# All activation products of a two-block transformer kernel read interleaved halves

## The reference

```
h = rmsnorm(x, norm)
x = x + (silu(h @ w_gate) * (h @ w_up)) @ w_down     # three times, 1024 -> 2816 -> 1024
q, k, v, ... = split(h @ w_in)                       # and the other projections, 1024 wide inputs
```

## Time and profile before

| | |
|---|---|
| Median of three timed runs | 1687.73 us |
| The profiled execution, its own time | 1688.09 us |
| Its span in the trace | 1686.3 us |
| TensorE matmul busy | 1664.0 us, 99% of the span, 10716 matmuls |
| TensorE weight loads busy | 1461.9 us, 87% |
| VectorE, ScalarE, GpSimd busy | 1259.2, 854.7, 527.4 us |
| TensorE clock granted, mean | 0.996 of full speed |

### The profile page before, as it was taken

How to read it: one execution, slowest core, us unless ns; L and a number is a source line. 1 busy time by engine, 2 the same in 40 slices (tenths; PEclk the granted TensorE clock), 3 DMA queues, 4 the chain that set the end, 5 groups by cost and what they waited for, 6 DMA issues and landing times.

```text
span 1686.3 us, 27591 instructions
## 1 busy us (share of the span) xinstructions
PE 1664.0 (99%) x10716; PEld 1461.9 (87%) x10716; DVE 1259.2 (75%) x1752; ACT 854.7 (51%) x1314; POOL 527.4 (31%) x368
## 2 busy tenths in 40 slices
PE   9989999999999999999999999999999999999997
PEld 7867789999998866789999998788888999899886
DVE  7767788845876798788855887688868975488675
ACT  6448457724763322557733774433335673277342
POOL 1451125503540446326502540121502560255000
PEclk9999999999999999999999999999999999999999
DMA  6310223433433565223344333422222333433432
GB/s 223 91 51 2 76 75 105 115 113 94 119 105 104 130 153 141 81 75 101 102 114 112 101 107 97 132 75 75 76 76 75 101 101 113 113 101 92 121 94 81
DMA packets 284923, 169.11 MB, mean 100 GB/s; under 512 B 8336, under 2 KB 278880, under 8 KB 284800
## 3 DMA queue, kind: packets, MB, share of 16 engines
q1 hardware_dynamic: 283792, 165.16, 34.8%
q0 software_dynamic: 720, 1.72, 0.3%
q10 hardware_dynamic: 288, 0.54, 0.1%
HBM read 156.71 MB, written 2.10 MB: 94 GB/s over the span
## 4 chain that ended last, share of the span: by engine, by line
PE 50%; DVE 4%; ACT 1%; issue 1%; DVEq 0%; ACTq 0%
PE ps L1454 22%; PE ps L1104 9%; PE ps L1106 9%; PE ps L1105 9%; DVE w L1803 1%; PE ps L1668 1%; ACT w L640 1%; DVE w L2131 0%; DVE act_lo L1835 0%; DVE bt_lo L1833 0%; DVE rstd L1845 0%; DVE tt L2147 0%; ACT w L810 0%; DVE x L2634 0%; PE ps L1681 0%
## 5 line engine op out<-in xcount | busy, mean ns | idle before, releaser
L1104 PE MATMUL ps<-act_hi,w 128*128 128x512 f32 x788 | 312.8, 397 | 3.8 <-DVE w L1803 2.3
L1106 PE MATMUL ps<-act_hi,w 128*128 128x512 f32 x788 | 307.0, 390 | 0.0
L1105 PE MATMUL ps<-act_lo,w 128*128 128x512 f32 x788 | 306.9, 390 | 0.0
L1454 PE MATMUL ps<-act_hi,w 128*128 128x256 f32 (+1 forms) x1461 | 270.3, 277 | 1.6 <-DVE w L2131 1.1
L640 ACT ACTIVATE w<-raw 128x2048 fp32r<-128x2048 f32 (+2 forms) x102 | 163.1, 1599 | 193.6 <-PE ps L1106 179.7
L1454 PEld LDWEIGHTS ps<-act_hi,w 128*128 128x128 f32 x1461 | 229.2, 188 | 3.3 <-DVE w L2131 1.7
L1803 DVE TENSOR_TENSOR w<-raw,w 128x2048 fp32r<-128x2048 f32 (+2 forms) x93 | 180.8, 1944 | 41.4 <-ACT w L640 41.3
L477 POOL TENSOR_TENSOR raw<-raw 128x512 f32<-128x512 f32 x60 | 81.9, 1365 | 405.4 <-DVE sqacc L1823 164.0
L1104 PE MATMUL ps<-hid_hi,w 128*128 128x512 f32 x528 | 200.1, 379 | 0.0
L1105 PE MATMUL ps<-hid_lo,w 128*128 128x512 f32 x528 | 200.1, 379 | 0.0
L1106 PE MATMUL ps<-hid_hi,w 128*128 128x512 f32 x528 | 200.1, 379 | 0.0
(11 more groups left out here) (430 smaller groups left out, 3595.6 us busy)
## 6 DMA issues: line engine op xcount, KB each, us to landing
raw<-in_ffn_w_gate_dram SPq DMA_DIRECT2D x44, 512.0 KB, 4.0
raw<-in_ffn_w_up_dram SPq DMA_DIRECT2D x44, 512.0 KB, 5.2
raw<-in_w_gate_upffn_dram SPq DMA_DIRECT2D x44, 512.0 KB, 4.5
raw<-in_ffn_w_down_dram SPq DMA_DIRECT2D x32, 384.0 KB, 4.2
raw<-in_conv_w_pw_dram SPq DMA_DIRECT2D x24, 512.0 KB, 5.7
raw<-in_w_in_dram SPq DMA_DIRECT2D x24, 512.0 KB, 4.4
raw<-in_ffn_w_down_dram SPq DMA_DIRECT2D x32, 320.0 KB, 3.7
z<-z SPq DMA_DIRECT2D x30, 262.0 KB, 4.9
```

The costliest lines, as they stand in the source:

```text
L1104: pe.matmul(out, lhs[0], rhs[0], start=start, stop=False)
L1105: pe.matmul(out, lhs[0], rhs[1], start=False, stop=False)
L1106: return pe.matmul(out, lhs[1], rhs[0], start=False, stop=stop)
L1454: ins = pe.matmul(out[:, c], lhs, rhs[:, k, c], start=start and k == 0 and rhs is b_hi and lhs is w_hi, stop=k == Q4 - 1 and lhs is w_lo, ...
```

## The change

Every product with activations now reads the columns in interleaved halves: those of 512 columns (`act_k`, and the embedding's `pf_hi`/`pf_lo`) in two halves of 256, the block products of 256 columns in two halves of 128. The output banks hold the tokens in that order, and each line that takes one out reads it with `in_turn` and writes with `by_half`. `act_hi` and `act_lo` become the two parts of one tile, `bt_hi` and `bt_lo` likewise. `HALVED` and the splitting in two pieces go.

```diff
-HALVED = (2, 3, 4, 7, 10, 12, 16)
...
-        act_hi = sb("act_hi", [P, KD, S], F32R)
-        act_lo = sb("act_lo", [P, KD, S], F32R)
+        act = sb("act", [P, 2, KD, S], F32R)
+        act_hi, act_lo = act[:, 0], act[:, 1]
...
+        def combo_tile(name, k):
+
+            if name in SUMS:
+                return bt[:, :, SUMS.index(name), k]
+            rows, cols = {"B11": (0, 0), "B21": (1, 0), "T4": (0, 1), "B22": (1, 1)}[name]
+            return act[:, :, rows * Q4 + k, cols * HALF:(cols + 1) * HALF]
...
-                dst = (a[:, 0:HALF], t2[:, u % 2, HALF:], t1[:, u % 2, HALF:])[i]
-                act.activation(dst, (c, b, a)[i][:, 0:HALF], ACT.Copy).then_inc(sem("taken"), 1)
+                src = (c, b, a)[i][:, 0:HALF]
+                if i:
+                    dst = by_half((t2, t1)[i - 1][:, u % 2, HALF:])
+                    act.activation(dst, in_turn(src), ACT.Copy).then_inc(sem("taken"), 1)
+                else:
+                    act.activation(a[:, 0:HALF], src, ACT.Copy).then_inc(sem("taken"), 1)
...
             def act_k(k):
-                return act_hi[:, k], act_lo[:, k]
+                return halves(act_hi[:, k]), halves(act_lo[:, k])
...
-                    def product(out, w, name, start, sig, halved=False):
-
-                        b_hi, b_lo = combo(name)
+                    def product(out, w, name, start, sig):
+
                         for k in range(Q4):
                             w_hi, w_lo = w(k)
+                            b_hi, b_lo = (halves(combo_tile(name, k)[:, j]) for j in range(2))
                             for lhs, rhs in ((w_hi, b_hi), (w_hi, b_lo), (w_lo, b_hi)):
-                                pieces = 2 if halved and k == 0 and lhs is w_lo else 1
-                                for i in range(pieces):
-                                    c = slice(i * HALF // pieces, (i + 1) * HALF // pieces)
-                                    ins = pe.matmul(out[:, c], lhs, rhs[:, k, c], start=start and k == 0
-                                                    and rhs is b_hi and lhs is w_hi, stop=k == Q4 - 1 and lhs is w_lo,
-                                                    skip_group_check=True)
+                                ins = pe.matmul(out[:, 0:HALF], lhs, rhs, start=start and k == 0 and rhs is b_hi
+                                                and lhs is w_hi, stop=k == Q4 - 1 and lhs is w_lo,
+                                                skip_group_check=True)
                         ins.then_inc(sig, 1)
...
-            def scaled(dst, src, parts=slice(0, P)):
-
-                ve.tensor_tensor(dst, src[parts, :], rstd[parts, :], ALU.mult).then_inc(bank_free, 1)
+            def scaled(dst, src):
+
+                ve.tensor_tensor(by_half(dst), in_turn(src), by_half(rstd[:, :]), ALU.mult).then_inc(bank_free, 1)
```

More of the change, by code:

```diff
@@ L1769, in ple @@
                     pe.wait_ge(sem("pf_done"), 2)
-                tile(T + 1, 4 * i, lambda k: slot(n, KD + k, P), lambda k: (pf_hi[:, k], pf_lo[:, k]), range(2),
+                tile(T + 1, 4 * i, lambda k: slot(n, KD + k, P), lambda k: (halves(pf_hi[:, k]), halves(pf_lo[:, k])), range(2),
                      panel_done)
@@ L1923, in _ @@
                     src = (second if c else first)("q", i)
-                    ve.scalar_tensor_tensor(out=q_f[:, 2 * i + c], in0=src[:, :], scalar=DH ** -0.5, in1=rstd[:, :],
-                                            op0=ALU.mult, op1=ALU.mult).then_inc(bank_free, 1)
+                    ve.scalar_tensor_tensor(out=by_half(q_f[:, 2 * i + c]), in0=in_turn(src), scalar=DH ** -0.5,
+                                            in1=by_half(rstd[:, :]), op0=ALU.mult, op1=ALU.mult).then_inc(bank_free, 1)
                 if i:
@@ L1976, in _ @@
             ve.wait_ge(panel_done, N0["gate"] + 1)
-            scaled(t3[:, 0], bank(T0["gate"]))
+            ve.tensor_tensor(t3[:, 0], bank(T0["gate"])[:, :], rstd[:, :], ALU.mult).then_inc(bank_free, 1)
             lo(N0["kvs"])
@@ L2076, in pooled @@
                 out, scale = ps[pool_banks[gi]], par[:, COL["pool_scale"] + gi:COL["pool_scale"] + gi + 1]
-                ve.tensor_scalar(act_hi[:, 4 + gi], out[:, :], scale, None, ALU.mult).then_inc(sem("y_hi"), 1)
-                low(act_lo[:, 4 + gi], out[:, :], act_hi[:, 4 + gi], "y_hi", gi + 1, "y_lo", scale)
+                ve.tensor_scalar(by_half(act_hi[:, 4 + gi]), in_turn(out), scale, None, ALU.mult)\
+                    .then_inc(sem("y_hi"), 1)
+                low(by_half(act_lo[:, 4 + gi]), in_turn(out), by_half(act_hi[:, 4 + gi]), "y_hi", gi + 1, "y_lo", scale)
             shift_first(0, 0)
@@ L2185, in gate_first @@
                         ve.wait_ge(sem("up_product"), 6 * seven(u) + 3)
-                        ve.tensor_tensor(t1[:, u % 2, 0:HALF], up_banks(dn, u)[2][:, 0:HALF], rstd[:, 0:HALF], ALU.mult)
+                        ve.tensor_tensor(by_half(t1[:, u % 2, 0:HALF]), in_turn(up_banks(dn, u)[2][:, 0:HALF]),
+                                         by_half(rstd[:, 0:HALF]), ALU.mult)
                     def gate_second(u):
@@ L2191, in gate_second @@
                         half = t1[:, u % 2, HALF:]
-                        seq.link(ve.tensor_tensor(half, half, up_banks(dn, u)[1][:, 0:HALF], ALU.add))
+                        seq.link(ve.tensor_tensor(by_half(half), by_half(half), in_turn(up_banks(dn, u)[1][:, 0:HALF]),
+                                                  ALU.add))
                         ve.tensor_tensor(half, half, rstd[:, HALF:], ALU.mult).then_inc(sem("up_summed"), 1)
@@ L2198, in up_second @@
                         half = t2[:, u % 2, HALF:]
-                        ve.tensor_tensor(half, half, up_banks(dn, u)[0][:, 0:HALF], ALU.add).then_inc(sem("c22_set"), 1)
+                        ve.tensor_tensor(by_half(half), by_half(half), in_turn(up_banks(dn, u)[0][:, 0:HALF]), ALU.add)\
+                            .then_inc(sem("c22_set"), 1)
                     def hidden(u, n):
@@ L2218, in whole_hidden @@
                         ve.wait_ge(sem("silu_ready"), u + 1)
-                        for half, sig in ((slice(0, HALF), "up_summed"), (slice(HALF, S), "hidden_set")):
-                            ve.tensor_tensor(t1[:, j, half], up_bank[:, half], t3[:, j, half], ALU.mult)\
+                        for h, sig in enumerate(("up_summed", "hidden_set")):
+                            half = slice(h * HALF, (h + 1) * HALF)
+                            ve.tensor_tensor(t1[:, j, half], in_turn(up_bank)[:, h], t3[:, j, half], ALU.mult)\
                                 .then_inc(sem(sig), 1)
@@ L2458, in _ @@
                     src = (second if c else first)("qk2", i)
-                    ve.scalar_tensor_tensor(out=dst[:, c], in0=src[:, :], scalar=1.0 if i else GDK ** -0.5,
-                                            in1=rstd[:, :], op0=ALU.mult, op1=ALU.mult).then_inc(bank_free, 1)
+                    ve.scalar_tensor_tensor(out=by_half(dst[:, c]), in0=in_turn(src), scalar=1.0 if i else GDK ** -0.5,
+                                            in1=by_half(rstd[:, :]), op0=ALU.mult, op1=ALU.mult).then_inc(bank_free, 1)
             lo(N0["v2"] + 1)
```

37 lines of the change are left out of this document (20 added, 17 removed).

## The result

The changed kernel takes 1661.85 us (median of four runs, 1659.99 to 1663.38), beside 1688.32 us (1687.16 to 1689.13) for the kernel before on the same chip: a ratio of 0.984, 95% interval 0.9827 to 0.9854. In a second session the pair stood at 1658.06 and 1688.26 us, 0.9829 (0.9814 to 0.9844). The forecast was 1655 us, in a range of 1640 to 1675. So the change saves 26.5 us in the first session and 30.2 in the second, where 32.5 had been worked out. The profiled execution took 1661.55 us, its span 1659.7.

What follows compares the result with a forecast made beforehand. TensorE, with matmuls in flight 99% of the span, was taken as the bound. 27.3 + 8.4 + 2.4 - 3.3 - 1.3 - 1.0 = 32.5 us off 1688.1 gave 1655.6, predicted as 1655 us, range 1640 to 1675.

Steps and rivals of the forecast that it cites:

- Products of 512 columns, 27.3 us: 2412 matmuls on `act` and `pf` go from 227.2 to 215.9 ns each, saving 27.3 us.
- Products of 256 columns, 8.4 us: 5040 block products go to 112.1 ns, from 113.2 or, for 620 of them, a slow 117.9: 8.4 us saved.
- The rival of 109.3 ns: Block products of 256 columns run at array speed, 109.3 ns, giving 1641 us; chance 0.14.
- the pace that sticks: Block products gain nothing, and without splits nothing ends their 117.9 ns pace: 1673 us; chance 0.18.
- the block products slower than 118.6 ns: Interleaved block products pay for changing lines; above 118.6 ns the change loses, at 122.6 ns 1708 us; chance 0.04.
- the rival that the 216 ns belong to the hidden tiles: Reading order doesn't matter, only the splits' time goes: 1686 to 1691 us; chance 0.04 together with the all-slow pace.
- Splits, 2.4 us: 21 split matmuls on TensorE cost 0.114 us each and go wholly: 2.4 us saved.
- Taking out, nothing: Strided reads of the output banks by VectorE and ScalarE were taken to cost nothing.
- Entries, 3.3 us given back: At three feed-forward entries TensorE waits for VectorE's chain, so the 96 matmuls beside it give back 1.1 us each time.
- Convolution and linear attention, 1.3 and 1.0 us: Where VectorE is nearly full, half the savings of 2.7 and 1.9 us are lost: 1.3 and 1.0 us.
- In the up products ... nothing lost.: VectorE's waits for TensorE at L2205 shrink by 0.1 of 0.8 us, so no time is given back there.
- rival 3: VectorE and ScalarE set the up products' pace, a slower `take` keeping the tile at 9.5 us: 1662 us; chance 0.10.

Runs made afterwards that it cites:

- experiment 4: Changed kernel; down products read in quarters, alternating pairs, even before odd; block products 192 columns in halves, 256 in quarters, 256 in order without splits: 1934.31 us.
- experiment 3: Kernel before the change with no split matmuls, everything still read in order: 1689.61 us, ratio 1.0001.
- experiments 1 and 2: Changed kernel with only the 512-column products interleaved, block products and splits as before: 1669.68 us; with only the 256-column block products interleaved, no splits: 1681.0 us.

## Why the prediction was right, and where it was not, point by point

- **Products of 512 columns, 27.3 us.** Right: 215.7 ns a step where 215.9 was taken, so 2412 x 11.3 stands. Reading the price off the down products, which had the same operand pattern, was enough.
- **Products of 256 columns, 8.4 us.** The step was taken at 112.1 ns and is 111.7: 4420 x 1.54 + 620 x 6.2 ns is 10.6 us. The slow pace did go entirely, as supposed. The reason was right as far as it can be seen: with 192 columns the step is the same (experiment 4), so the columns don't set it; that the weight load does is not shown. The rival of 109.3 ns fell, and so did the pace that sticks, the block products slower than 118.6 ns, and the rival that the 216 ns belong to the hidden tiles.
- **Splits, 2.4 us.** Confirmed as a cost. That they also did something, end the slow pace, shows in experiment 3.
- **Taking out, nothing.** Right: 376 against 374 ns on ScalarE, 686 against 686 on VectorE.
- **Entries, 3.3 us given back.** The mechanism was right and experiments 1 and 2 show it. Its size: the first two tiles take 21.99 us where 21.34 less 0.28 and 0.36 were due, 1.3 us for each entry, 3.9 in all. What I left out is that a gain in these two tiles themselves is given back as well.
- **Convolution and linear attention, 1.3 and 1.0 us.** They were 2.7 and 1.8. In the convolution layer the clock cost 3.4 us before and after, so the 2.7 are waits (the longest, for GpSimd's L564, went from 0.8 to 2.3 us), and as much as what the 240 matmuls beside a full VectorE could save at all, not half of it. In the linear attention 1.7 of the 1.8 is a fall of the clock that the profile of before doesn't have.
- **Not in the sum at all.** The attention layer gave back 1.8 us and the embedding 0.8 (to which waits was not followed further). I had looked at windows where VectorE is full and took it that everywhere else TensorE sets the pace.
- **"In the up products ... nothing lost."** This is the step that failed, and it had the wrong wait as the cover. The waits of VectorE at L2205 did not shrink by 0.1 us of 0.8: in the trace 18.4 us are left of 34.6, and 17 waits of 43. The room was taken by waits behind ScalarE, which the list of waits shows (us in total, times, longest):

```profile
DVE sw_lo L2144 <- ACT ps L829: 40.0, 54, 1.2
DVE w L2138 <- ACT w L815: 30.5, 35, 1.2
```

The same two were 31.4 and 18.9 us before: VectorE stands as long as it did, but at ScalarE's door. And L2205 (now L2216) could not have been the cover. It waits for the T4 product, and T4 (`fourth`) itself waits until VectorE has done `up_second` (L2199, now L2209). What covered TensorE was the wait of `up_second`, which is much smaller, before and after:

```profile
DVE t L2199 <- PE ps L1454: 11.3, 29, 0.5
```

```profile
DVE t L2209 <- PE ps L1460: 5.2, 12, 0.5
```

TensorE's listed waits within the block products don't show this loss. They add up to 5.0 us, 1.9 before, with four entries

```profile
PE ps L1460 <- ACT t L841: 1.4, 6, 0.3
PE ps L1460 <- issue: 1.4, 3, 0.5
PE ps L1460 <- DVE w L2138: 1.3, 3, 0.4
...
PE ps L1460 <- ACT ps L843: 0.7, 3, 0.2
```

and all of them are the five waits of the entry, three times over; only 0.2 us lie elsewhere, at L2209. The loss is in the distances of the starts. From the fourth tile of a feed-forward on (counted as before, from the first that is made of block products), 16 of 51 tiles take 0.07 to 0.43 us more than their full pace (9.45 to 9.76 us for one of 9.38), 3.2 us in all; in the second profile they are 11 tiles and 2.0 us. In each of the 16, `up_second` ends 1.25 us or more after the tile's first matmul; in none of the other 35 does it end later than 1.18 us, and in none of the 51 of the kernel before later than 1.15 us. A late tile and the one behind it:

```profile
278.16 1.29 POOL L490 TENSOR_TENSOR ssum<-raw,ssum 128x512 f32<-128x512 f32 x1
278.72 2.88 DVE L2138 TENSOR_TENSOR w<-raw,w 128x2048 fp32r<-128x2048 f32 x1 [1.14 <-ACT w L815]
...
283.54 0.41 DVE L2209 TENSOR_TENSOR t<-t,ps 128x256 f32<-128x256 f32 x1
284.00 1.41 PEld L1460 LDWEIGHTS ps<-act,w 128*128 128x128 f32 x12 [0.30 <-DVE t L2209]
...
286.32 1.52 POOL L490 TENSOR_TENSOR ssum<-raw,ssum 128x512 f32<-128x512 f32 x1
288.47 2.29 DVE L2138 TENSOR_TENSOR w<-raw,w 128x2048 fp32r<-128x2048 f32 x1 [1.14 <-ACT w L815]
```

Both times VectorE starts the split of the weights (L2138) as late as ScalarE lets it. The first time GpSimd's sum (L490) still runs, the split takes 2.88 us instead of 2.29, and T4's weights are loaded only when `up_second` is done. The rule in the traces is exact: over all 180 such splits of the kernel before and of both profiles of the changed one, the duration is 2.29 us, or 2.15 us plus the time that a GpSimd instruction runs beside it if that is more, within 0.01 us. All 16 late tiles have a stretched split (2.56 us or more). So a tile is late when VectorE starts late behind ScalarE and GpSimd's sum falls into the split as well. Before, splits were stretched as often (33 over 2.45 us, against 26 and 31 after), but VectorE started them earlier in the tile. GpSimd's chain starts at a weight transfer in 38 of the 60 tiles of the first profile; why that falls differently in each execution was not followed, and no run moved GpSimd's sum.

The terms again, forecast and measured in the first profile: 27.3 and 27.5 (what the table's 40.5 leave for the 512 columns); 8.4 and 10.6; 2.4 and 2.4; entries -3.3 and -3.9; convolution -1.3 and -2.7; linear attention -1.0 and -1.8; attention layer and embedding 0 and -2.6; later tiles 0 and -3.0 (what the feed-forwards' 6.9 leave, beside the 3.2 counted above). That is 32.5 and 26.5. The second profile has 1.2 us less in the later tiles and 2.4 less in the convolution layer. Its last matmul starts at 1647.80 us, 30.1 us ahead of the kernel before. Of 40.5 us that the distances alone were worth, two thirds came through, on an engine that is busy 99% of the time.

The first session's 1661.85 us is the number of rival 3 (1662 us, VectorE and ScalarE set the pace of the up products), but not its case: L841 stays at 376 ns, and 35 of the 51 tiles run at TensorE's own pace. VectorE and ScalarE, with GpSimd, do set the other 16. The distances' gain was taken 2.4 us too low and what is given back 8.4 us too low. That the first error makes up for part of the second, and leaves 6.0 us, is luck.

**The rule that spoke against it.** Halves 16 bytes, 64 bytes and 1 KB apart all run at 216 ns for 512 columns. The Trainium skill ("Advanced Engine Details and Errata", Memory Cachelines) says that an access to another line of 16 bytes each time is penalised. For the halves no run here shows that, and the measurement decides: they are 11.3 ns faster than the order of the memory. For the quarters (283 ns) and for every fourth element (461), which also go to another 16 bytes each time, the trace agrees in sign. Every second element (451) and the pairs (333) read twice in a row in the same 16 bytes, which by the same section of the Trainium skill is enough to hide the memory's latency; the trace does not agree, both are slower than the order of the memory (227).

## What to carry to other kernels

Look in the trace for two groups of the same size that differ in one thing only; the 5% between the distances on `hid` and `act` gave this change and its price. For fp32 data in this fast form, the moving operand read as two interleaved halves is the fastest order of those tried, it may have the halves as close as 16 bytes, and putting the columns back in order cost VectorE and ScalarE nothing here when they take out the bank. When the bounding engine gets a little faster, the cover is the helper's wait just before the signal that this engine needs next (here `up_second`, 11.3 us in 29 of 60 tiles), tile by tile; a longer wait behind that signal (L2205, 34.6 us) covered nothing here. Here a third of the gain went in many small waits. Some of them are too short for the list of waits and show only in the distances of the starts.

## What was not expected of the hardware

- The distance of 512-column matmuls by the order of reading: two halves 216 ns, in order 227, four quarters 283, pairs alternating between the halves 333, every second element 451, every fourth 461.
- With a new 128x128 weight tile for each, a matmul of 192 and one of 256 columns start at the same distance, 111.7 ns. Ordered reads of 256 columns have 113.2 or 117.9 for long stretches, and the kernel enters the second near the start of a feed-forward, in some of them and not in others.
- The clock fell to its lower level for stretches of 3.41 or 6.83 us. After one and the same 2.3 us wait it did so in one execution and not in two others.
- VectorE's split of a weight tile (128 by 2048, 2.29 us by itself) was held up while a GpSimd instruction ran: 0.72 us side by side made it 2.87 us, 0.94 us made it 3.09.
